# Attention scores as three rounded products with stacked key parts, score units of three blocks in two halves

## The reference

```python
dots = jnp.einsum('bthd,bsd->bths', qi, ki_all)
score = jnp.einsum('bth,bths->bts', wi, jax.nn.relu(dots))
score = jnp.where(allowed[None], score, -jnp.inf)
top_val, top_idx = lax.top_k(score, topk)          # topk = 256
kg = gather(k_all, top_idx)
vg = gather(v_all, top_idx)
logits = jnp.einsum('btngd,btknd->btngk', qg, kg) * (HEAD_DIM ** -0.5)
p = jax.nn.softmax(logits, axis=-1)
o = jnp.einsum('btngk,btknd->btngd', p, vg)
```

## Time and profile before

| | |
|---|---|
| Runs, median (lowest to highest) | 3011.31 us (3008.76 to 3017.05) |
| Profiled execution, its own time | 3008.23 us |
| Its span in the profile | 3006.5 us |
| Mean granted clock of PE | 0.985 |
| PE busy | 2856.5 us, 95% |
| DVE busy | 1643.6 us, 55% |
| ACT busy | 987.3 us, 33% |
| POOL busy | 648.8 us, 22% |

### The profile page before, as it was taken

The page is one execution under the profiler, slowest core; times in us unless marked ns, Lnnn a source line. Parts: engine busy times, 40 slices in busy tenths (PEclk is TensorE's granted clock), DMA queues, the critical chain, the costliest instruction groups (busy, mean ns, idle before and its releaser), DMA issues.

```text
span 3006.5 us, 43059 instructions
## 1 busy us (share of the span) xinstructions
PE 2856.5 (95%) x16186; PEld 2453.2 (82%) x16186; DVE 1643.6 (55%) x2804; ACT 987.3 (33%) x1260; POOL 648.8 (22%) x280
## 2 busy tenths in 40 slices
PE   5999889999999999999989989899999999999997
PEld 2778733379999999999977876234999999999996
DVE  7758777785452534524544777763435344344355
ACT  4246646533221111111233565563332111121112
POOL 2411410011222222222242034000112212222221
PEclk9999999999999999999999999999999999999999
DMA  5412100242222222212241311002112222222222
GB/s 218 138 64 85 37 22 1 57 162 84 84 84 70 84 70 84 86 54 85 76 135 47 123 43 37 1 1 64 43 64 91 64 76 80 73 84 72 82 83 86
DMA packets 71352, 224.95 MB, mean 75 GB/s; under 512 B 17232, under 2 KB 17488, under 8 KB 70096
## 3 DMA queue, kind: packets, MB, share of 16 engines
q1 hardware_dynamic: 70192, 219.36, 21.7%
q10 hardware_dynamic: 1056, 4.19, 0.3%
HBM read 211.44 MB, written 11.54 MB: 74 GB/s over the span
## 4 chain that ended last, share of the span: by engine, by line
PE 42%; issue 32%; DVE 11%; ACT 7%; POOL 4%; DVEq 2%; DMA 1%; ACTq 0%; POOLq 0%; SPq 0%
PE ps L980 33%; ACT notsel L779 5%; POOL w_lo L617 4%; PE ps L1238 2%; DVE smax L1732 1%; PE ps L1222 1%; PE ps L1031 1%; DVE hf L1389 1%; DMA w_ada<-in_w_ada 1%; PE ps L1226 1%; PE ps L1206 1%; DVE s_cand L1519 1%; DVE s_keep L1531 1%; PE ps L1228 1%; PE ps L1094 1%
## 5 line engine op out<-in xcount | busy, mean ns | idle before, releaser
L617 POOL TENSOR_TENSOR w_lo<-w_raw,w_hi 128x1024 fp32r<-128x1024 f32 x202 | 500.4, 2477 | 1852.8 <-ACT w_hi L730 1852.8
L980 PE MATMUL ps<-u_hi,w_hi 128*128 128x352 f32 (+1 forms) x2112 | 457.5, 325 | 2.1 <-ACT rstd L931 2.1
L980 PE MATMUL ps<-u_hi,w_lo 128*128 128x352 f32 (+1 forms) x2112 | 458.4, 325 | 0.0
L980 PE MATMUL ps<-u_lo,w_hi 128*128 128x352 f32 (+1 forms) x2112 | 455.6, 324 | 0.0
L730 ACT CAST w_hi<-w_raw 128x1024 fp32r<-128x1024 f32 x202 | 211.0, 1045 | 528.4 <-PE ps L980 337.7
L980 PEld LDWEIGHTS ps<-u_hi,w_hi 128*128 128x128 f32 x2112 | 362.1, 189 | 3.7 <-ACT rstd L931 2.7
L980 PEld LDWEIGHTS ps<-u_lo,w_hi 128*128 128x128 f32 x2112 | 361.0, 189 | 0.0
L980 PEld LDWEIGHTS ps<-u_hi,w_lo 128*128 128x128 f32 x2112 | 360.9, 189 | 0.0
L779 ACT ACTIVATE notsel<-score,s_cand 128x384 bf16<-128x384 f32 (+3 forms) x248 | 297.5, 1200 | 139.3 <-DVE s_cand L1519 139.1
L1830 DVE SCALAR_TENSOR_TENSOR x<-ps,mod,x 128x704 f32 (+2 forms) x240 | 125.5, 579 | 347.5 <-PE ps L980 341.1
L980 PE MATMUL ps<-a_hi,w_hi 128*128 128x352 f32 x1056 | 228.7, 325 | 4.3 <-POOL w_lo L617 2.1
(11 more groups left out here) (265 smaller groups left out, 4152.5 us busy)
## 6 DMA issues: line engine op xcount, KB each, us to landing
w_ada<-in_w_ada SPq DMA_DIRECT2D x96, 512.0 KB, 4.8
w_raw<-in_w_up SPq DMA_DIRECT2D x88, 512.0 KB, 3.4
w_raw<-in_w_in SPq DMA_DIRECT2D x34, 512.0 KB, 3.5
cw<-in_convw SPq DMA_DIRECT2D x32, 512.0 KB, 5.1
ada_later<-in_w_ada SPq DMA_DIRECT2D x24, 512.0 KB, 3.6
w_raw<-in_w_down SPq DMA_DIRECT2D x32, 384.0 KB, 3.1
w_raw<-in_w_down SPq DMA_DIRECT2D x32, 320.0 KB, 2.9
w_raw<-in_w_out SPq DMA_DIRECT2D x16, 512.0 KB, 3.5
```

The costliest lines, as they stand in the source:

```text
L617: nc.gpsimd.tensor_tensor(w_lo[slot][:], w_raw[:], w_hi[slot][:].bitcast(F32), ALU.subtract)\
L980: last = nc.tensor.matmul(ps[:, bank + t, 0:w], wt[slot][:, kk, :], mv[:, kk, t * TW:t * TW + w], start=(at == 0 and p == 0), stop=(at == ...
```

## The change

For blocks 2 to 7 the float32 product of q and k becomes three products of rounded parts (fp32r). With hi the rounded part and lo the rest, q k is taken as q_hi k_hi + q_hi k_lo + q_lo k_hi. `k_two[n]` holds k_hi of group n in its own 64 rows and k_lo in the other 64; `q_two[i][:, n]` holds q_hi in both halves. One product of 128 rows (full height) then gives the first two terms, and a half-height pair of `q_lo` and `k_two` the third. Blocks 0 and 1 and the sample keep float32.

The parts are made once a layer. ACT rounds (two casts of 64 x 1024 for k, two of 64 x 4 x 128 for each of the six blocks), POOL subtracts (`k_lo` twice, `q_lo` twice a block, with drains), and SP copies on the chip the halves that are to stand twice (two transfers of 256 KB for k, two of 128 KB for each block). The copies of q_two(2), q_two(3), k_two and q_two(4 to 7) stand in that order on SP ahead of its wait for the gates.

```diff
+SPLIT = {3: 1, 4: 2, 5: 3}
+def units_of(i):
+    of_l = [("L", n) for n, x in enumerate(L_UNITS) if x[0] == i + 1]
+    of_s = [("S", n) for n, x in enumerate(S_UNITS) if x[0] == i]
+    if i not in SPLIT:
+        return of_l + of_s
+    return of_l[:4] + of_s[:SPLIT[i]] + of_l[4:] + of_s[SPLIT[i]:]
...
-SEARCH_BEHIND = {2: (0, 1), 3: (0, 2), 4: (0, 2, 3), 5: (0, 2, 3, 4), 6: (0, 1)}
+SEARCH_BEHIND = {2: (0, 1, 2), 3: (2, 3), 4: (2, 3, 4), 5: (3, 4, 5), 6: (0, 1)}
...  SP
+                def double_queries(i):
+                    sp.wait_ge(q_high.sem, q_high.at(l, i - 1))
+                    settle(sp)
+                    sp.dma_start(q_two[i][64:128, 0].bitcast(F32), q_two[i][0:64, 0].bitcast(F32)).then_inc(q_doubled[i].sem, 16)
+                    sp.dma_start(q_two[i][0:64, 1].bitcast(F32), q_two[i][64:128, 1].bitcast(F32)).then_inc(q_doubled[i].sem, 16)
...
                 sp.wait_ge(c_ready.sem, c_ready.at(l, 2))
+                sp.wait_ge(pv_used.sem, pv_used.at(l, N_S))
...  POOL
+                def queries_low(i):
+                    pool.wait_ge(q_high.sem, q_high.at(l, i - 1))
...
+                        last = nc.gpsimd.tensor_tensor(q_lo[r, :, at], q[r, :, at], q_two[i][r, n].bitcast(F32), ALU.subtract)
...
+                gate(0)
+                pool.wait_ge(k_high.sem, k_high.at(l, 1))
...
+                    last = nc.gpsimd.tensor_tensor(k_lo[r, :], k[r, 0:SEQ], k_two[n][r, :].bitcast(F32), ALU.subtract)
+                last.then_inc(k_low.sem, 1)
+                queries_low(2)
+                gate(1)
+                for i in range(3, QB):
+                    queries_low(i)
...  ACT
+                        last = nc.scalar.copy(q_two[i][r, n], q[r, :, i * P:(i + 1) * P])
...
+                    last = nc.scalar.copy(k_two[n][r, :], k[r, 0:SEQ])
+                last.then_inc(k_high.sem, 1)
+                queries_high(2)
+                act.wait_ge(sp_ready.sem, sp_ready.at(l, 2))
+                queries_high(3)
...
+                act.drain()
+                for i in range(4, QB):
+                    queries_high(i)
                 nc.scalar.preload_act_table_set(LN_EXP)
...
-                    if kb == 0:
-                        for _ in range(SEARCH_IN.get(i + 1, 0)):
+                    between = SEARCH_IN.get(i + 1, 0)
+                    if i in SPLIT:
+                        between = {0: between - 2, SPLIT[i]: 1}.get(kb, 0)
+                    elif kb:
+                        between = 0
...
                     exponentials(t, P, PLACE["S", t], 512)
+                    if i in SPLIT and kb == 0:
+                        count(searched, [PSRCH])
...  PE, logits units (the S units in the same way)
+                        for n in range(2):
+                            nc.tensor.matmul(ps[:, bank + n, 0:w], q_two[i][:, n, b, :], k_two[n][:, c:c + w], start=True, stop=False)
+                        for n in range(2):
+                            nc.tensor.matmul(ps[:, bank + n, 0:w], neg_ident[:, 0, :], selection(i, c, w), start=False, stop=False)
+                        for n in range(2):
+                            r = slice(64 * n, 64 * n + 64)
+                            last = nc.tensor.matmul(ps[:, bank + n, 0:w], q_lo[r, b, i * P:(i + 1) * P], k_two[n][r, c:c + w],
+                                                    start=False, stop=True)
```

86 lines of the change are left out of this document (71 added, 15 removed).

## The result

| | before | changed |
|---|---|---|
| Median of the runs | 3013.55 us (4 runs) | 3034.15 us (4 runs, 3030.47 to 3040.49) |
| Ratio, 95% interval | | 1.0081 (1.0056 to 1.0105) |
| Profiled execution, its span | 3006.5 us | 3028.7 us |

The changed kernel is 0.8% slower, 20.6 us by the medians and 22.2 us by the two profiled spans. The forecast was 18 us, and 3034.15 us lies within its range of 3002 to 3043. The sum came out nearly right, but three of its four terms did not, as the next sections show.

What follows compares the result with a forecast made beforehand. PE, busy 95% of the span, was taken as the bound, though attention also waits for DVE and ACT. Per layer 9.0 - 10.3 + 8.6 + 1.8 = 9.1 us, 18 in both, gave 3028 us, range 3002 to 3043.

Steps and rivals of the forecast that it cites:

- The late first selection: DVE's chain before the first selection waits for POOL's operations under way; selection and PE 9 us late per layer.
- 9 us of waiting for sel_ready: Sign to look for: PE's wait before the first selected unit about 9 us instead of 0.18.
- The products: Rounded products in the attention's logits and S units, 0.19 us less per 512-key unit; -10.3 us of PE work per layer.
- Leaving and entering the half-height shape: Within each half-height pair on PE, 0.21 us for going into and out of the shape.
- That the two products of a pair run side by side: Rounded half-height pair on PE costs one stream of 0.213 plus 0.21 us, 0.42, as the float32 pair does.
- The stops: PE's stops from first selection to last product grow from 15.5 to 24.1 us, +8.6 per layer.
- the nine foretold stops: PE stops behind the first selection of 3.4, 2.7, 1.7, 4.4, 2.7, 1.3, 2.7, 1.1 and 1.7 us, in program order.
- The clock: One more stretch at 1.2 instead of 2.4 GHz after PE's stops, +1.8 us per layer.
- One reading at the prediction's start: PE is busy 95% of the span, and the chain that ended last lies mostly in it.
- That the products decide: First rival: DVE's small operations slip between POOL's and the split offsets the counts; 2988 to 2994 us, chance 0.14.
- That DVE is not held up: Second rival: POOL does not delay DVE, but the stops grow; 3008 to 3014 us, up to 3020, chance 0.20.
- That the rounded pair runs one product after the other: Third rival, with POOL starving DVE as alternative: +3 to +12 us per layer on the forecast, 3034 to 3050, chance 0.13.

Runs made afterwards that it cites:

- e4: Kernel before's float32 products and order, with the rounded parts made and waited for but unused; 3027.1 us, ratio 1.0056.
- e10: As e4, with each of POOL's 14 subtractions cut to one column; 3010.9 us, ratio 1.0007.
- e5: As e1, with the third product at full height from the stacked parts, q_lo k_hi left out; 3016.8 us, ratio 1.0023.
- e2: Kernel before with only the split of the logits units and the moved counts; 3016.4 us, ratio 1.0026.
- e1: Changed kernel without the split and with the counts where they stood before, so rounded products and preparation alone; 3028.9 us, ratio 1.0064.
- e13: Changed kernel with POOL's subtractions cut to one column, third product reading rounded queries instead of low parts; 3018.6 us, ratio 1.0030.
- e8: As e1, with the mask pair of each logits unit of blocks 2 to 7 issued twice, result the same; 3026.5 us, ratio 1.0062.

## Why the prediction was right

**The late first selection: 9 forecast; DVE's chain 7.9 and 8.0 longer, the head 6.1 and 7.0.** The mechanism, the place and the direction were right: e4 has the whole of it, e10 none. What is missing from the 9 lies in the assumption that each operation meets a subtraction just begun: line 1673 fell into the 0.16 us between a subtraction and the gate and passed in 0.16 us, and line 1670 met the end of a subtraction and took 0.68. The sign named for it, 9 us of waiting for sel_ready, did not come (1.62 us), because PE waited 5.55 us for a maximum inside the chain first. The predicated copy was held up (2.27 us). The prediction took it that the Trainium skill ("SBUF — State Buffer", Who interferes with whom) leaves this operation out and put 8 to its account. The page doesn't name it, but its rule on instructions with two SBUF inputs covers it: the row has s_keep and s_cand as inputs, and the trace agrees.

**The products: -10.3 forecast; -4.2 and -4.6 of work measured, and it did not reach the time.** Here the step failed. Leaving and entering the half-height shape was taken as 0.21 us a pair. It is that and 0.13 more before the next full-height product (0.58 for 0.45), and the full-height shape throughout (e5) takes this away. Layer 0's units of 512 gained 0.06 and 0.05 us instead of 0.19. A narrow unit of 128 columns got 0.12 us longer (0.76, from 460.33 to 461.09, for 0.64 from 443.18 to 443.82), where the forecast had some 0.2. Right behind a product with the values such a unit takes 1.05 us (457.75 to 458.80), but there the values product ahead of it takes 1.39 us up to the unit's start (456.36 to 457.75) where it took 1.91 (441.27 in the earlier trace rows to 443.18), so the two together are 2.44 us for 2.55. The rule of the Trainium skill ("TensorEngine Tiling (Array Packing)", Key Properties) that a change of tiling mode drains the engine points at this cost and gives it no number. By e5 the drain and the pair together cost 0.17 us against one shape throughout. That the two products of a pair run side by side was right: the pair takes 0.26 us at 128 columns (458.54 to 458.80) and 0.43 at 512 (563.20 to 563.63), 0.17 more for 384 columns. One stream of 384 columns at 2.4 GHz would be 0.16, two would be 0.32.

```profile
456.36 1.96 PE L1353 MATMUL ps<-probs,vaug 128*128 128x512 f32 x4
457.75 0.73 PE L1303 MATMUL ps<-k_two,q_two 128*128 128x128 f32 x2
...
458.54 0.33 PE L1308 MATMUL ps<-k_two,q_lo 64*128 64x128 f32 x2
458.80 0.73 PE L1303 MATMUL ps<-k_two,q_two 128*128 128x512 f32 x2
...
460.33 0.44 PE L1303 MATMUL ps<-k_two,q_two 128*128 128x128 f32 x2
...
461.09 0.73 PE L1331 MATMUL ps<-q_two,k_two 128*128 128x512 f32 x2
```

```profile
443.18 0.49 PE L1206 MATMUL ps<-k,q 64*128 64x128 f32 x4
...
443.82 1.13 PE L1206 MATMUL ps<-k,q 64*128 64x512 f32 x4
```

**The stops: +8.6 forecast.** From the second selection's wait on, the stops of 0.25 us or more in the changed kernel are 3.10, 1.43, 0.29, 1.42, 4.13, 2.02, 0.67, 0.45, 2.27, 0.63 and 1.58, together 18.0 us. The forecast's 24.1 counted small stops too, the 15.5 before did not; with those of 0.25 us and more it is 16.1, so the stops grew by 1.9. All idle time of the body grew by 3.9 us, and by 2.0 in layer 1. The places and the origins of the nine foretold stops are right, but the one for probs in block 2 is 0.29 us instead of 2.7 (1.51 in layer 1), and the others are shorter than foretold. In e2, with the longer float32 products, the same order added only 0.7 and 1.1 us of idle time; in e5, with less work, idle time grew. That fits the reading that less work between the stops lengthens them, and that this term was high because the products' term was, but no run tests it by itself.

**The clock: +1.8 forecast, 5.1 and 8.5 more lost** (8.5 and 11.9 us for 3.4), of which 3.6 and 7.0 us fall on PE's busy time; in the old order (e1) 12.0 and 10.2 more. The term was taken from the stretches of the kernel before and did not ask what one-pass products between the stops do to it.

**The sum.** Forecast 9.0 - 10.3 + 8.6 + 1.8 = 9.1. Measured in layer 0: 6.1 in the head and 3.3 in the body, which are 3.9 of idle time, 3.6 of clock and -4.2 of work, together 9.4; in layer 1 7.0 and 2.0 + 7.0 - 4.6, together 11.4. The direction rests on a mechanism that held, POOL's work beside DVE. That the number came so near is luck: the products gave 6 us less than forecast, and the stops took 5 to 7 us less. In the old order, where the forecast would have given -1.3 a layer, the errors would not have met: e1 lies 22 us above that.

One reading at the prediction's start is too strong: the chain that ended last lies in PE for 42% of the span, with 32% of issue, not mostly in it. Nothing of the sum hangs on it.

**The rivals.** That the products decide (2992) fell: even at no price for preparation (e13) the kernel is slower, and against e4 the products alone (e1) bring no time. That DVE is not held up fell with e4 and e10. That the rounded pair runs one product after the other fell with 1.54 us for the unit. I had not listed that the clock could eat the products' gain.

What stays open: why the clock falls more often among half-height rounded products. That it does is shown (8.5 to 18.8 us lost a layer in the bodies of the kernels with them, but for e8; 0 to 8.5 with float32), and that added full-height work undoes it (e8), but not what in them does it: their shape, as e5 suggests, or how little PE has to do between two stops. And whether the moved order is better than the old one for the rounded products: the profiled bodies are 244.0 / 245.1 and 247.4 / 246.0, but of the fastest execution of one and the slowest of the other, and by the ratios (1.0081 and 1.0064, with intervals that overlap) the two cannot be told apart.
